# Two of eight weighted sums of a conditioning projection move from VectorE to TensorE in a fused mixer and MoE layer

## The chip, the cores and the metric

The kernel runs on one core of a Trainium2 chip. The time is device microseconds (us) of one execution, and the figure to compare is the median of several runs.

## The reference, cut to what matters

One layer of a decoder: 256 tokens of width 1024, float32. A condition vector `c` modulates both halves of the layer, then a mixer and a mixture of 32 experts (4 per token) follow.

```python
cond = jax.nn.silu(c)
mod = (cond @ w_ada[l] + b_ada[l])[:, None, :]                 # 1024 -> 6 * 1024
sh_m, sc_m, g_m, sh_f, sc_f, g_f = jnp.split(mod, 6, axis=-1)
h = modulate(rms_norm(x, norm_mix_g[l]), sh_m, sc_m)
x = x + g_m * hybrid_mixer(h, w_in[l], ..., w_out[l])
h = modulate(rms_norm(x, norm_ffn_g[l]), sh_f, sc_f)
y = moe_ffn(h.reshape(-1, d), router_w[l], ...)                # top 4 of 32 experts
x = x + g_f * y.reshape(bsz, seq, d)
return rms_norm(x, final_norm_g)
```

The change concerns the last third of `cond @ w_ada`: the 2048 columns that hold `sc_f` and `g_f`, a sum over 1024 rows.

## The kernel before, in words

**Two stages.** The mixer multiplies the tokens with `w_in` (7 sections of 1024 columns) and `w_out`. The experts then stream their weights, 6 units of 2 MB each, through 12 buffers. Nearly everything that is computed is small against the 466 MB that are read.

**The mixer's weights** come in units of 2 MB (or 1 MB, a "half") through four buffers R0 to R3 in `raw` and a few places aside; the list `homes` (L61) gives the order and the home of each. SP issues all loads in that order and waits before each until the former user of the place is done: for units of `w_in` on the semaphore `split_l`, for units of `w_ada` on `ada_used` (L412 to L440). A wait on SP holds every later load.

**Products.** ScalarE copies a weight piece rounded (`piece_high`, L627), VectorE makes the rest (`piece_low`, L831, which counts `split_l`), and TensorE takes three products per block (L1192). A step of the mixer is numbered m = 0 to 23: 2 column halves h, times 6 sections (`SC_C, SC_X, SC_B, GATE_A, U_, GATE_B`), times 2 pieces b. So m = 12 to 23 is h = 1, m = 18 and 19 are its GATE_A, m = 20 and 21 its U. The bank of step m is `B[m % 6]`. In iteration m VectorE and ScalarE first make piece m + 3, which needs TensorE to be through with step m, and then treat the bank of step m. The multiplication with `w_out` (L1423 with its helper L1192, banks `B[0]` to `B[3]`) follows step 23.

**The conditioning product on the side.** The first third is a TensorE product (`modulation`, L1222). The second is weighed on VectorE: each row of weights times its own scalar of `cT`, added up (`weigh`, L881 and L882), and TensorE adds the 128 partitions with a matrix of ones (`sum_weighed`, L1244). The last third comes in eight halves of 128 rows by 2048 columns: half 0 is weighed on ScalarE (L701), halves 1 to 7 on VectorE (`weigh_half`, L893), in the iterations that `HALF_AT` names (L78). The running sum is the left half of `spare`. After iteration 20 `sum_weighed(2)` adds its partitions into `B[0]` with 4 products, one for each 512 columns, which lie in four column groups of 32. VectorE then adds the bias (L826). Half 6 lies in the right half of `spare`, half 7 in the left half of R2.

**Hand over to the experts.** The first loads of expert weights wait on the end of the mixer. SP issues, in this order (L474 and on): load 0 once VectorE has made all pieces of U (`split_l`), load 1 once all halves are used (`ada_used` 16), the two pieces of `w_out`'s second half (L464) once the spatial products are done (`sp_done` 4), load 2 once `sum_weighed(2)` is done, load 3 once the pieces of GATE_B are made, load 4 and 5 on the first pieces of `w_out` and on step 23, load 6 on the last piece of the mixer's result, load 7 and 8 on parts of the `w_out` product, load 9 and 10 on its end (`mix_done` 4, the last product of TensorE in the mixer), and load 11 behind the router (`spread_out` 4). Each is 2 MB. After that each load waits for a buffer that TensorE releases (L1508 are the products of the experts).

Of the kernel before, what the change touches and what calls it, by code (L numbers as in the profile page):

```python
# [5 lines left out]
def hybrid_trunk(nc, x_in, c_in, w_ada, b_ada, norm_mix_g, w_in, conv_w, w_spatial, b_spatial, ln_v_g,  # L6
# [31 lines left out]
    KT = D // P  # L38
    HALF = 512
    NH = D // HALF  # L40
# [10 lines left out]
    SC_X, SC_B, SC_C, U_, V_, GATE_A, GATE_B = range(7)  # L51
# [23 lines left out]
    units = [u for u, _ in homes]  # L75
    TABLES_MIX, TABLES_FFN = ("ada", 1, 1), ("ada", 1, 2)
    WEIGH_AT = {1: 0, 4: 1, 7: 2, 9: 3}
    HALF_AT = {12: (1, 2), 13: (3,), 15: (4,), 16: (5,), 17: (6,), 18: (7,)}  # L78
    SUM_AT = {11: 1, 20: 2}
    HALVES = 2 * NS * NH  # L80
    split_units = [n for n, u in enumerate(units) if u[0] in ("in", "out")]
# [10 lines left out]
    unit_no = {u: n for n, u in enumerate(units)}  # L92
# [5 lines left out]
    with ctx:  # L98
# [3 lines left out]
        def sem(name):  # L102
            return ctx.enter_context(nc.semaphore(name))
# [20 lines left out]
        weighed = spare[:, 0:4 * HALF].rearrange("p (j n) -> p j n", j=4)  # L124
# [13 lines left out]
        def slot(n, k=1):  # L138
            return W[:, n * UW:(n + k) * UW]
# [12 lines left out]
        cond = late[:, 5 * P:5 * P + KT * 32].rearrange("p (k r) -> p k r", k=KT)  # L152
# [114 lines left out]
        ada_used = sem("ada_used"); weighed_ready = sem("weighed_ready"); ada_summed = sem("ada_summed"); ones_ready = sem("ones_ready"); split_h = sem("split_h"); split_l = sem("split_l")  # L267
# [15 lines left out]
        sec_act = sem("sec_act")  # L283
# [43 lines left out]
        def dve_bank(h, s, b):  # L327
            return dve_order.index((h, s, b)) + 1
# [4 lines left out]
        def act_bank(h, s, b):  # L333
            return act_order.index((h, s, b)) + 1

        def home(n):
            return homes[n][1]

        def raw_slot(n):
            if home(n) == ASIDE_SPARE:  # L340
                return spare[:, :]
            if home(n) == ASIDE_M:
                return slot(7)
            if home(n) == SPARE_RIGHT:
                return spare[:, UW // 2:UW]
            if home(n) in (R2_LEFT, R2_RIGHT):
                at = R2 * UW + (UW // 2 if home(n) == R2_RIGHT else 0)
                return raw[:, at:at + UW // 2]
            return raw[:, home(n) * UW:(home(n) + 1) * UW]

        def landed(n):
            return s_slot[home(n)], 16 * len([m for m in range(n + 1) if home(m) == home(n)])
# [22 lines left out]
        def sum_bank(i):  # L375
            return B[7] if i == 1 else B[0]
# [419 lines left out]
        def _(dve):  # L796
# [74 lines left out]
            def weigh(q):  # L871

                n = unit_no[("ada", 1, q)]
                dve.wait_ge(*landed(n))
                if q == 0:
                    dve.wait_ge(split_l, pieces_before[split_units.index(unit_no[("in", SC_X, 0)]) + 1])
                w = raw_slot(n).rearrange("p (k j n) -> p k j n", k=2, j=4)
                if q == 0:
                    step(V.tensor_scalar(weighed[:, :, :], w[:, 0], cT[:, 0:1], None, ALU.mult))
                else:  # L880
                    step(V.scalar_tensor_tensor(weighed[:, :, :], w[:, 0], cT[:, 2 * q:2 * q + 1], weighed[:, :, :], ALU.mult, ALU.add))  # L881
                V.scalar_tensor_tensor(weighed[:, :, :], w[:, 1], cT[:, 2 * q + 1:2 * q + 2], weighed[:, :, :], ALU.mult, ALU.add).then_inc(ada_used, 1)  # L882
                dve.wait_ge(ada_used, 4 + q + 1)
                if q == 3:
                    dve.nop().then_inc(weighed_ready, 1)

            def weigh_half(j):

                n = unit_no[("half", 2, j)]
                dve.wait_ge(*landed(n))  # L890
                dve.wait_ge(ada_used, 8 + j)
                sum_of = spare[:, 0:UW // 2]
                V.scalar_tensor_tensor(sum_of, raw_slot(n), cT[:, j:j + 1], sum_of, ALU.mult, ALU.add).then_inc(ada_used, 1)  # L893
                dve.wait_ge(ada_used, 8 + j + 1)
                if j == KT - 1:
                    dve.nop().then_inc(weighed_ready, 1)

            piece_low(V_ALL)
# [22 lines left out]
            for h in range(NH):  # L921
                for n, s in enumerate(SECTIONS):
                    for b in range(2):
                        m = 2 * (NS * h + n) + b
# [11 lines left out]
                        if s == SC_X:  # L936
# [6 lines left out]
                            for t in (2 * b, 2 * b + 1):  # L943
                                k = 4 * h + t
                                w = [cols[:, KT * (1 + j) + k:KT * (1 + j) + k + 1] for j in range(3)]
# [29 lines left out]
                        if m in WEIGH_AT:  # L975
                            weigh(WEIGH_AT[m])
                        for j in HALF_AT.get(m, ()):
                            weigh_half(j)
# [199 lines left out]
        def _(pe):  # L1178
            M = nc.tensor.matmul
# [3 lines left out]
            def arrived(n):  # L1183
                pe.wait_ge(*landed(n))

            def piece_ready(q):
                pe.wait_ge(split_l, q + 1)

            def product(o, k, left, right):

                for n, (i, j) in enumerate(((0, 0), (0, 1), (1, 0))):
                    t = M(o, left[i], right[j], start=(k == 0 and n == 0), stop=(k == KT - 1 and n == 2))  # L1192
                return t
# [31 lines left out]
            def turn_sums(part, g):  # L1225
# [4 lines left out]
                    t = M(first_bank(part, g)[:, q:q + 1], mod[:, g, P * q:P * q + P], row_sum, start=True, stop=True)  # L1230
                t.then_inc(modT_done, 1)

            def sum_weighed(i):

                if i == 1:
                    pe.wait_ge(wsT_ready, 2)
                    pe.wait_ge(ones_ready, 1)
                if i == 1:
                    pe.wait_ge(sp_used, 2)
                else:  # L1240
                    pe.wait_ge(sec_act, act_bank(NH - 1, GATE_A, 0))
                pe.wait_ge(weighed_ready, i)
                for j in range(4):
                    t = M(sum_bank(i)[32 * j:32 * j + 32, :], cond[:, 0, :], weighed[:, j, :], start=True, stop=True)  # L1244
                t.then_inc(ada_summed, 1)

            modulation(0, 0)
# [1 line left out]
            for k in range(KT):  # L1249
                for a in range(TA):  # L1250
                    c = T * (k % 2) + P * a
                    t = TR(B[k // 2][:, c:c + P], HV[:, a, k * P:(k + 1) * P], ident[:, :])
# [60 lines left out]
            def spatial(c):  # L1313

                if c == 0:
                    pe.wait_ge(v_ready, TA)
                    pe.wait_ge(wsT_ready, 2)
                if c >= 2:
                    pe.wait_ge(sp_used, c - 1)
                if c == 3:  # L1320
                    pe.wait_ge(mod_ready, 1)
                for g in (2 * c, 2 * c + 1):
                    for a in range(TA):
                        o = T * (g % 2) + P * a
                        t = M(B[6 + c % 2][:, o:o + P], HV[:, a, g * P:(g + 1) * P], wsT[:, g, :], start=True, stop=True)
                t.then_inc(sp_done, 1)


            for h in range(NH):
                for i, s in enumerate(SECTIONS):  # L1330
                    for b in range(2):
                        if s == U_ and b == 0:
                            spatial(2 * h)
                            spatial(2 * h + 1)
                        m = 2 * (NS * h + i) + b
                        if m >= 4 and m < 6:
                            pe.wait_ge(v_gelu, m - 3)
                        if m >= 6:
                            m0 = m - 6
                            h0, s0, b0 = m0 // (2 * NS), SECTIONS[(m0 // 2) % NS], m0 % 2  # L1340
                            if s0 in (SC_X, SC_B):
                                pe.wait_ge(sec_dve, dve_bank(h0, s0, b0))
                            else:
                                pe.wait_ge(sec_act, act_bank(h0, s0, b0))
                        q = V_ALL + m
                        piece_ready(q)
                        for tt in range(2):
                            for k in range(KT):
                                cs = slice(P * tt, P * tt + P)
                                t = product(B[m % 6][:, T * tt:T * tt + T], k, (in_set(wh, q)[:, k, cs], in_set(wl, q)[:, k, cs]),  # L1350
                                            (hh[:, k, :], hl[:, k, :]))
                        t.then_inc(sec_done, 1)
                        if m in SUM_AT:
                            sum_weighed(SUM_AT[m])
                    if s == SC_B and h == 0:
                        turn_spatial()
# [36 lines left out]
            for h in range(NH):  # L1393
                for ks in ((range(0, 4), range(4, 6), range(6, 8)) if h == 0 else (range(0, 4), range(4, 8))):
# [3 lines left out]
                    for a in range(TA):  # L1398
                        for k in ks:
# [3 lines left out]
                            t = product(B[TA * h + a][:, :], k, (mh[:, k, ts], ml[:, k, ts]), (rows_h[:, k % 4, :], rows_l[:, k % 4, :]))  # L1403
# [15 lines left out]
                    if h == 0 and ks[0] == 0:  # L1419
                        pe.wait_ge(sec_act, act_bank(NH - 1, GATE_B, 1))  # L1420
                        pe.wait_ge(sp_used, NG // 2)
                        for q in range(QW):
                            t = TR(B[6][:, P * q:P * q + P], mod[:, 1, P * q:P * q + P], ident[:, :])  # L1423
# [59 lines left out]
            for a in range(TA):  # L1483
                t = TR(B[7][:, a * P:(a + 1) * P], wts4[:, a, :], ident[:, :])
# [100 lines left out]
            n = pe.snap(rnd, min_val=0, max_val=ALL_ROUNDS)  # L1585
# [6 lines left out]
            n = pe.snap(rnd, min_val=0, max_val=ALL_ROUNDS)  # L1592
# [28 lines left out]
```

## Time and profile before

| | |
|---|---|
| median of 3 runs | 1139.98 us (1139.22 to 1141.19) |
| profiled execution, its own time | 1139.67 us |
| span of that execution in the profile | 1137.9 us |
| TensorE busy | 962.7 us (85%) |
| VectorE busy | 352.1 us (31%) |
| DMA queue of SP, share of the 16 engines | 98.8% |
| read from memory | 465.35 MB, 410 GB/s over the span |

The page gives busy time, a row of 40 slices (28.4 us each) for every engine, and the chain of waits that ended last. The busy shares say little alone, since the first 220 us and the rest are different programs; the slices and the chain, read against the order of loads above, tell which resource holds each stage.

### The profile page before, as it was taken

What the parts mean: (1) busy time and instruction counts of PE and PEld (TensorE: products, weight loads), DVE (VectorE), ACT (ScalarE), POOL (GpSimd) and SP (SyncE); (2) the same over time, 40 slices, a digit from 0 to 9 for tenths busy, and PEclk for the clock granted to TensorE, in tenths of its full rate; (3) what the DMA queues carried; (4) which work ended last, traced back from release to release, by engine and by line L of the source; (5) the groups of instructions that cost most, each with busy time, mean ns of one, the idle gap of its engine ahead of it and who ended that gap; (6) DMA issues with size and microseconds to landing.
All of it is one profiled execution on the core that took longest, in us unless ns stands there. A gap on an engine that the chain in (4) does not pass through costs nothing.

```text
span 1137.9 us, 24483 instructions
## 1 busy us (share of the span) xinstructions
PE 962.7 (85%) x10064; PEld 511.7 (45%) x10065; DVE 352.1 (31%) x799; ACT 248.1 (22%) x369; POOL 8.2 (1%) x30
## 2 busy tenths in 40 slices
PE   7999999989887997798898888989887687687664
PEld 6799999734332333243333334434333233233221
DVE  3688996752121222121222212212121121121112
ACT  3644535521011111010111101111010010111102
POOL 0010000000000000000000000000000000000000
PEclk9999999999999999899999999999989899899988
DMA  9999889999999999999999999999999999999996
GB/s 358 395 354 359 320 333 375 416 389 430 427 428 429 427 429 427 428 427 427 430 426 429 427 429 425 430 425 429 428 429 429 427 429 426 427 429 428 429 426 273
DMA packets 56094, 466.79 MB, mean 410 GB/s; under 512 B 5252, under 2 KB 6340, under 8 KB 27396
## 3 DMA queue, kind: packets, MB, share of 16 engines
q1 hardware_dynamic: 55808, 466.12, 98.8%
q8 instruction: 19, 0.31, 0.1%
q10 hardware_dynamic: 260, 0.30, 0.1%
q14 instruction: 7, 0.06, 0.0%
HBM read 465.35 MB, written 1.05 MB: 410 GB/s over the span
## 4 chain that ended last, share of the span: by engine, by line
PE 53%; DMA 39%; issue 3%; SPq 2%; DVE 1%; ACT 1%; PEld 0%; PEldq 0%; POOL 0%; POOLq 0%; DVEq 0%; ACTq 0%
PE B L1508 25%; DMA trio<-in_w_down_dram 25%; PE B L1192 14%; DMA W<-in_w_down_dram 10%; DMA W<-in_w_gate_up_dram 3%; PE B L1532 3%; PE B L1521 2%; SPq L474 2%; PE B L1460 2%; PE B L1271 1%; PE B L1466 1%; PE B L1199 1%; PE B L1280 1%; PE B L1222 0%; PE B L1566 0%
## 5 line engine op out<-in xcount | busy, mean ns | idle before, releaser
L1508 PE MATMUL B<-W,trio 128*32 128x512 f32 (+1 forms) x4768 | 469.9, 530 | 125.5 <-DMA W<-in_w_gate_up_dram 52.1
L1508 PEld LDWEIGHTS B<-W,trio 128*32 128x32 f32 x4768 | 154.9, 111 | 368.2 <-issue 225.0
L751 ACT ACTIVATE EW<-EW 128x256 f32<-128x256 f32 x46 | 19.1, 416 | 680.3 <-DVE EW L1124 680.3
L1124 DVE TENSOR_SCALAR EW<-B 128x256 f32<-128x256 f32 x46 | 19.5, 425 | 447.3 <-PE B L1508 447.3
L1192 PE MATMUL B<-hh,wh 128*128 128x256 f32 x384 | 109.1, 284 | 0.0
L1192 PE MATMUL B<-hl,wh 128*128 128x256 f32 x384 | 108.7, 283 | 0.0
L1192 PE MATMUL B<-hh,wl 128*128 128x256 f32 x384 | 108.7, 283 | 0.0
L1532 PE MATMUL B<-EW,trio 32*128 32x256 f32 x752 | 67.1, 426 | 8.7 <-PE B L1532 7.8
L1192 PEld LDWEIGHTS B<-hh,wh 128*128 128x128 f32 x384 | 73.7, 192 | 1.7 <-issue 1.7
L1192 PEld LDWEIGHTS B<-hl,wh 128*128 128x128 f32 x384 | 73.7, 192 | 0.0
L1192 PEld LDWEIGHTS B<-hh,wl 128*128 128x128 f32 x384 | 73.7, 192 | 0.0
L1139 DVE TENSOR_TENSOR EW<-B,trio 128x256 f32<-128x256 f32 x46 | 19.5, 425 | 164.7 <-PE B L1508 164.7
L627 ACT ACTIVATE wh<-raw 128x2048 fp32r<-128x2048 f32 (+1 forms) x30 | 50.3, 1690 | 83.0 <-PE B L1192 66.8
L831 DVE TENSOR_TENSOR wl<-raw,wh 128x2048 fp32r<-128x2048 f32 (+1 forms) x30 | 59.9, 2004 | 14.8 <-ACT wh L627 14.1
L1508 PE MATMUL B<-trio 128*32 128x256 f32 x768 | 48.6, 395 | 15.2 <-DMA trio<-in_w_down_dram 15.2
L751 ACT ACT_TABLE_LOAD x46 | 59.0, 1283 | 6.1 <-issue 5.3
L1521 PE MATMUL B<-b_gu,trio 128*32 128x256 f32 x736 | 56.4, 423 | 0.0
L1508 PE MATMUL B<-spare,trio 128*32 128x512 f32 x352 | 46.9, 647 | 8.2 <-DMA spare<-in_w_gate_up_dram 8.2
L1460 PE MATMUL B<-HV,trio 128*32 128x256 f32 x752 | 51.7, 388 | 0.0
L1532 PEld LDWEIGHTS B<-EW,trio 32*128 32x128 f32 x752 | 29.4, 182 | 47.4 <-PE B L1532 26.6
L1521 PEld LDWEIGHTS B<-b_gu,trio 128*32 128x32 f32 x736 | 29.3, 116 | 43.8 <-issue 38.0
L1460 PEld LDWEIGHTS B<-HV,trio 128*32 128x32 f32 x752 | 28.8, 113 | 38.9 <-issue 32.4
(259 smaller groups left out, 709.0 us busy)
## 6 DMA issues: line engine op xcount, KB each, us to landing
W<-in_w_gate_up_dram SPq DMA_DIRECT2D x112, 2048.0 KB, 33.7
W<-in_w_down_dram SPq DMA_DIRECT2D x48, 2048.0 KB, 37.4
spare<-in_w_gate_up_dram SPq DMA_DIRECT2D x16, 2048.0 KB, 37.1
trio<-in_w_down_dram SPq DMA_DIRECT2D x15, 2048.0 KB, 40.4
raw<-in_w_in_dram SPq DMA_DIRECT2D x10, 2048.0 KB, 14.5
raw<-in_w_ada_dram SPq DMA_DIRECT2D x4, 2048.0 KB, 16.9
raw<-in_w_ada_dram SPq DMA_DIRECT2D x7, 1024.0 KB, 11.8
raw<-in_w_in_dram SPq DMA_DIRECT2D x4, 1024.0 KB, 15.6
```

The lines of the kernel that those rows point to most:

```text
L474: sp.dma_start(unit_pair(u).rearrange("p g n -> p (g n)"), dn_v[e, j - NQ].rearrange("p g n -> p (g n)")).then_inc(s_unit[u % SLOTS], 16)
L627: A(in_set(wh, q), in_raw(q), ACT.Copy).then_inc(split_h, 1)
L751: A(sg, gs, ACT.Sigmoid, scale=ALPHA).then_inc(sig_ready, 1)
L831: V.tensor_tensor(in_set(wl, q), in_raw(q), in_set(wh, q).bitcast(f32), ALU.subtract).then_inc(split_l, 1)
L1124: V.tensor_scalar(halves(gs), paired(GU[:, 0:QC]), LIMIT, None, ALU.min).then_inc(gmin_ready, 1)
L1139: V.tensor_tensor(yw, Db[:, 0:QC], gfq, ALU.mult).then_inc(yw_ready, 1)
L1192: t = M(o, left[i], right[j], start=(k == 0 and n == 0), stop=(k == KT - 1 and n == 2))
L1199: TR(bank[:, 0:P], ident[:, :], ident[:, :])
L1460: t = M(Db[CAP * g:CAP * g + CAP, 0:QC], S[:, a, CAP * g:CAP * g + CAP], HV[:, a, g * QC:(g + 1) * QC], start=(a == 0), stop=(a == TA - 1))
L1508: t = M(o, src[:, k % KQ, CAP * (k // KQ):CAP * (k // KQ) + CAP], w, start=(k == 0), stop=(k == KT - 1))
L1521: M(GU[CAP * g:CAP * g + CAP, s * QC:(s + 1) * QC].rearrange("p (c q) -> p c q", q=KQ), sel[:, NH * s + g // 2, :], pairs[:, :, g % 2, :], ...
L1532: M(Yb[a][h][:, (g % 2) * QC:(g % 2) * QC + QC], SwT[rows_, a * P:(a + 1) * P], yw[rows_, :], start=False, stop=True, skip_group_check=Tru ...
```

## The change

Halves 6 and 7 are no longer weighed on VectorE. TensorE multiplies them with `cond` in 8 products (128 rows by 512 columns, in the same four column groups), straight into the bank that `sum_weighed(2)` adds to afterwards. They stand right behind the products of step 19, ahead of the spatial products. `ada_used` 15 and 16, for which SP waits, are now counted by TensorE. The running sum on VectorE is complete after half 5, and `sum_weighed(2)` adds to the bank in place of starting it.

```diff
-    HALF_AT = {12: (1, 2), 13: (3,), 15: (4,), 16: (5,), 17: (6,), 18: (7,)}
+    HALF_AT = {12: (1, 2), 13: (3,), 15: (4,), 16: (5,)}
+    PRODUCTS_OF, PRODUCTS_AT = (6, 7), 19
...
-                if j == KT - 1:
+                if j == PRODUCTS_OF[0] - 1:
                     dve.nop().then_inc(weighed_ready, 1)
...
+            def half_products():
+
+                pe.wait_ge(sec_act, act_bank(NH - 1, GATE_A, 0))
+                pe.wait_ge(ada_used, 8 + PRODUCTS_OF[0])
+                for j in PRODUCTS_OF:
+                    n = unit_no[("half", 2, j)]
+                    arrived(n)
+                    w = raw_slot(n).rearrange("p (i n) -> p i n", i=4)
+                    for i in range(4):
+                        t = M(sum_bank(2)[32 * i:32 * i + 32, :], cond[:, j, :], w[:, i, :], start=(j == PRODUCTS_OF[0]), stop=False)
+                    t.then_inc(ada_used, 1)
+
             def sum_weighed(i):
...
                 if i == 1:
                     pe.wait_ge(sp_used, 2)
-                else:
-                    pe.wait_ge(sec_act, act_bank(NH - 1, GATE_A, 0))
                 pe.wait_ge(weighed_ready, i)
                 for j in range(4):
-                    t = M(sum_bank(i)[32 * j:32 * j + 32, :], cond[:, 0, :], weighed[:, j, :], start=True, stop=True)
+                    t = M(sum_bank(i)[32 * j:32 * j + 32, :], cond[:, 0, :], weighed[:, j, :], start=(i == 1), stop=True)
                 t.then_inc(ada_summed, 1)
...
                         t.then_inc(sec_done, 1)
+                        if m == PRODUCTS_AT:
+                            half_products()
                         if m in SUM_AT:
                             sum_weighed(SUM_AT[m])
```

VectorE, iterations 17 to 19 (`spare` is the running sum, `wl` the piece that VectorE makes, L951 the bank of SC_B, L955 that of GATE_A), before:

```order
L951 TENSOR_TENSOR tmp<-tmp,B 128x512
L893 SCALAR_TENSOR_TENSOR spare<-spare,tmp 128x2048
L831 TENSOR_TENSOR wl<-raw,wh 128x2048
L955 TENSOR_TENSOR tmp<-tmp 128x512
L893 SCALAR_TENSOR_TENSOR spare<-raw,tmp,spare 128x2048
L831 TENSOR_TENSOR wl<-raw,wh 128x2048
L955 TENSOR_TENSOR tmp<-tmp 128x512
L831 TENSOR_TENSOR wl<-raw,wh 128x2048
```

and now (each line number is one higher):

```order
L952 TENSOR_TENSOR tmp<-tmp,B 128x512
L832 TENSOR_TENSOR wl<-raw,wh 128x2048
L956 TENSOR_TENSOR tmp<-tmp 128x512
L832 TENSOR_TENSOR wl<-raw,wh 128x2048
L956 TENSOR_TENSOR tmp<-tmp 128x512
L832 TENSOR_TENSOR wl<-raw,wh 128x2048
```

The two weighings are gone; each stood ahead of a piece that SP or TensorE waits for. TensorE from the last product of step 19 to the first of step 20, before (`B<-tmp,HV` are the spatial products):

```order
L1192 MATMUL B<-hh,wl 128x256
L1325 MATMUL B<-tmp,HV 128x128 [waits sp_used]
L1325 MATMUL B<-tmp,HV 128x128 x3
L1325 MATMUL B<-tmp,HV 128x128 [waits mod_ready,sp_used]
L1325 MATMUL B<-tmp,HV 128x128 x3
L1192 MATMUL B<-hh,wh 128x256 [waits split_l,sec_dve]
```

and now (`s_slot8` is the landing of half 6, `s_slot6` that of half 7):

```order
L1193 MATMUL B<-hh,wl 128x256
L1243 MATMUL B<-spare,tmp 32x512 [waits s_slot8,ada_used,sec_act]
L1243 MATMUL B<-spare,tmp 32x512 x3
L1243 MATMUL B<-raw,tmp 32x512 [waits s_slot6]
L1243 MATMUL B<-raw,tmp 32x512 x3
L1336 MATMUL B<-tmp,HV 128x128 [waits sp_used]
L1336 MATMUL B<-tmp,HV 128x128 x3
L1336 MATMUL B<-tmp,HV 128x128 [waits mod_ready,sp_used]
L1336 MATMUL B<-tmp,HV 128x128 x3
L1193 MATMUL B<-hh,wh 128x256 [waits split_l,sec_dve]
```

Eight products stand ahead of all that follows on TensorE, with three new kinds of wait.

## Rows read from the trace of the kernel before

**Rows 1.** The page: DMA rate in 40 slices of 28.4 us.
```profile
GB/s 358 395 354 359 320 333 375 416 389 430 427 428 429 427 429 427 428 427 427 430 426 429 427 429 425 430 425 429 428 429 429 427 429 426 427 429 428 429 426 273
```
**Rows 2.** The chain that ended last, in order of time: start us, us, what.
```profile
30.30 1.85 PE B L1222 x16
...
124.30 46.27 PE B L1192 x384
...
170.57 1.79 PE B L1325 x16
...
178.10 0.99 PE B L1244 x8
...
235.04 3.00 PE B L1508 x16
...
269.14 33.45 DMA trio<-in_w_down_dram
```
**Rows 3.** Timeline of VectorE, 162 to 175 us.
```profile
162.02 2.35 DVE L893 SCALAR_TENSOR_TENSOR spare<-raw,tmp,spare 128x2048 f32<-128x2048 f32 x1
...
167.33 2.35 DVE L893 SCALAR_TENSOR_TENSOR spare<-spare,tmp 128x2048 f32<-128x2048 f32 x1
169.72 2.29 DVE L831 TENSOR_TENSOR wl<-raw,wh 128x2048 fp32r<-128x2048 f32 x1
...
172.53 2.34 DVE L893 SCALAR_TENSOR_TENSOR spare<-raw,tmp,spare 128x2048 f32<-128x2048 f32 x1
```
**Rows 4.** Timeline of ScalarE: the piece of iteration 18 and the bank of step 18.
```profile
164.90 1.92 ACT L627 ACTIVATE wh<-raw 128x2048 fp32r<-128x2048 f32 x1 [3.84 <-PE B L1192]
166.73 0.58 ACT L696 ACTIVATE tmp<-B 128x512 f32<-128x512 f32 x1
```
**Rows 5.** Timeline of TensorE around `sum_weighed(2)`.
```profile
177.70 0.28 PE L1192 MATMUL B<-hl,wh 128*128 128x256 f32 x1
177.82 0.28 PE L1192 MATMUL B<-hh,wl 128*128 128x256 f32 x1
178.03 1.06 PE L1244 MATMUL B<-spare,tmp 128*32 128x512 f32 x8
...
179.25 0.28 PE L1192 MATMUL B<-hl,wh 128*128 128x256 f32 x1
```
**Rows 6.** Timeline of SP: half 7, loads 0, 1, 8, 9 and 11.
```profile
159.08 0.33 SPq L440 DMA_DIRECT2D raw<-in_w_ada_dram  x1
...
172.03 0.33 SPq L470 DMA_DIRECT2D W<-in_w_gate_up_dram  x1
...
174.90 0.33 SPq L470 DMA_DIRECT2D W<-in_w_gate_up_dram  x1
...
216.00 0.33 SPq L470 DMA_DIRECT2D W<-in_w_gate_up_dram  x1
...
222.36 0.33 SPq L470 DMA_DIRECT2D W<-in_w_gate_up_dram  x1
...
231.58 0.67 SPq L472 DMA_DIRECT2D trio<-in_w_down_dram  x1
```
**Rows 7.** DMA issues, us to landing: half 7, loads 0, 8, 9, 11.
```profile
raw<-in_w_ada_dram SPq DMA_DIRECT2D x1, 1024.0 KB, 5.0
...
W<-in_w_gate_up_dram SPq DMA_DIRECT2D x1, 2048.0 KB, 7.7
...
W<-in_w_gate_up_dram SPq DMA_DIRECT2D x1, 2048.0 KB, 9.9
...
W<-in_w_gate_up_dram SPq DMA_DIRECT2D x1, 2048.0 KB, 8.9
...
trio<-in_w_down_dram SPq DMA_DIRECT2D x1, 2048.0 KB, 10.0
```
**Rows 8.** Busy time by stretch; the last number is the DMA rate in GB/s.
```profile
170.00:175.00 5.00, 5.00 (x45) 5.00 (x44) 4.87 (x3) 2.52 (x2) 0.00 (x0) 1.00 0.42 108
220.00:225.00 5.00, 4.78 (x47) 3.64 (x46) 3.06 (x6) 2.66 (x8) 0.00 (x0) 1.00 0.97 360
```

## The prediction, on record before the changed kernel ran

> **What bounds the kernel now.** I read the slices first. From slice 9 on the DMA rate stays at 425 to 430 GB/s, while before it, in the mixer, it lies between 320 and 416 [rows 1]. So the experts' stage (some 880 us of it) runs at the rate of the loads, and nothing that TensorE or VectorE saves there counts. What counts is when this stream gets going and whether it is ever interrupted before.
>
> Next the chain of waits [rows 2]. Through the second half of the mixer it runs on TensorE alone: 46.27 us without a break for steps 12 to 19 (384 products in 46.1 us is 5.76 us a step), the spatial products and `sum_weighed(2)`, each followed by further steps. The end of the `w_out` product sends load 9 at 222.36 [rows 6]. TensorE starts the first expert at 235.04, and only at 269.14 does the chain pass to a load, one that takes 33.45 us to land behind the loads queued ahead of it. Up to about 245 us the loads are issued as TensorE gets on; after that they queue and the rate alone decides.
>
> Then VectorE around the change [rows 3]. It weighs half 6 at 167.33 (2.35 us) and only then makes its piece of iteration 18 at 169.72, though ScalarE's part of that piece was ready at 164.90 + 1.92 = 166.82 [rows 4]. It weighs half 7 at 172.53, to 174.87. SP waits for both: load 0 goes out at 172.03, as the piece ends, and load 1 at 174.90, as half 7 is weighed [rows 3, 6]. The queue has run dry by then, with 108 GB/s between 170 and 175 us [rows 8]. That is the hole which this change can fill.
>
> **What the change removes.** Two VectorE operations, 2.35 + 2.34 = 4.7 us. The piece of iteration 18 can start at 167.33 in place of 169.72, so load 0 goes out 2.4 us earlier, at 169.65. The next piece waits for ScalarE, whose step needs TensorE's step 19 anyway; TensorE never waited for a piece in this stretch (its 5.76 us a step has no gap), so VectorE's freed time gives TensorE nothing.
>
> **What it adds on TensorE.** Eight products of 128 by 512 in column groups, which the trace lists as 16 records. The nearest row is `sum_weighed(2)`: four of the same form, 8 records. Without them the last product at 177.82 would be followed 0.12 us later by the next (the distance from the row before), and one product after that stands at 179.25. So 179.25 - 177.82 - 2 x 0.12 = 1.19 us is the whole price of four, both changes of form included [rows 5]. `modulation` has eight such products at 1.85 us, against 0.99 us for four [rows 2], so four more cost 0.86 us. Together 1.19 + 0.86 = **2.05 us**. From below the price is 1.85 us, the eight alone; from above it is 2 x 1.19 = 2.4 us, if half 6 and half 7 are paid for like two separate groups. I take 2.05, since the two stand back to back as in `modulation`.
>
> The Trainium skill (TensorEngine Tiling (Array Packing), Key Properties) says that changing the tiling mode drains TensorE, which speaks against putting short products in column groups between full ones. By the rows above the two changes and the drain are worth 1.19 - 0.86 = 0.33 us, which the sum has. The page gives no figure for it, so by the rule alone the term could not be sized.
>
> **Waits.** All that the eight products wait for is long there when step 19 ends at 170.4: half 5 is weighed at 162.02 + 2.35 = 164.4 [rows 3], the bank of step 18 is read at 167.3 [rows 4], half 7 has landed at 159.08 + 5.0 = 164.1 [rows 6, 7], and half 6 was there at 167.33, when VectorE took it [rows 3]. I price them at nothing. If one were late, it would hold the spatial products, the remaining steps and everything else on TensorE.
>
> **What moves.** The products end near 172.4, where `ada_used` reaches 16; load 1 leaves at about 172.6, 2.3 us earlier than now. The `w_out` pieces then wait for the spatial products, which end at 172.4 now [rows 2] and at 174.4 then, still ahead of load 1's present 174.9. Load 2 waits for `sum_weighed(2)` and is later by 2.05, after 181.1 in place of 179.1 [rows 2]; it is covered by loads 0 and 1 and the `w_out` pieces, 6 MB or about 15 us. Everything that waits for a later step of TensorE, loads 3 to 11 and the router among it, moves back by 2.05 us.
>
> **The sum.** Does the stream feel the 2.4 us gained at load 0, or the 2.05 us lost behind it? Load 8 goes out at 216.00 and lands at 225.9; load 9 goes out at 222.36, on the last product of TensorE in the mixer, and lands at 231.3 [rows 6, 7]. That is 5.4 us apart, where 2 MB at 427 GB/s take 4.9, and the rate in that stretch falls to 360 GB/s [rows 8]. Load 11 goes out at 231.58 and lands at 241.6, where two loads of 4.9 us behind load 9 would be down at 231.3 + 9.8 = 241.1. So both come late already today: what the queue had been given earlier is used up by load 9, and the head start of 2.4 us only makes it wait longer there. From load 9 on the whole stream moves with TensorE. Terms: VectorE 0 (hidden under TensorE's steps), load 0 and 1 0 (spent before load 9), TensorE +2.05, router and experts 0. The profiled execution of 1139.67 us would come to 1141.7; the median lies 0.3 above that execution, so I predict **1142.0 us**, with 1141.8 to 1142.4 by the bounds of the one term, and 0.6 us of scatter on either side, as runs lie up to 1.2 us above their median.
>
> **Rivals.**
>
> *The wait is hidden at load 9.* Load 0, into an empty queue, landed in 7.7 us [rows 7]. If load 9 needs no more than that, it lands at 222.36 + 2.05 + 7.7 = 232.1, 0.8 us later than now and not 2.05. With load 11 soaking up some of it in the same way, the sum lies between 0 and +0.8: 1140.0 to 1140.8. For it: 8.9 is more than 7.7. Against it: the dip in rate at 220 to 225, and load 11, which again comes late and is again tied to TensorE. The Trainium skill (DMA: Bandwidth & Descriptors, Anatomy of one DMA) fits the gpsimd path with 2.0 us plus bytes over 436 GB/s, 6.8 us for 2 MB as an estimate; by that load 9 would land at 231.2, just as now, and the change would cost nothing. SP's loads here need 7.7 us even alone. Chance 0.16.
>
> *The head start carries.* If the late landings of loads 9 and 11 are only a lower rate of the engines and not late issues, then the queue holds work throughout, and all later loads keep the 2.3 us that loads 0 and 1 gain: 1139.98 - 2.3 = 1137.7 us, faster. It decides from the point where load 4 to load 9 never find the queue short. Against it: load 9's lead over the landing of load 8 is 3.5 us now and would be no larger than that. Chance 0.07.
>
> *The products cost more in this place, and the kernel is slower.* Between step 19 and step 20 stand three kinds of products in a row now, half 6, half 7 behind a landing wait and a count of its own, and the spatial ones. If the overlap breaks at each of the three borders and each costs what the break at `sum_weighed(2)` costs, it is 3 x 1.19 = 3.6 us: 1143.6. It decides from 2.3 us on, where the shift exceeds what can be told. For it: none of the rows has such a sequence. Against it: `modulation` runs eight such products in 1.85 us, and its two groups of four overlap. Chance 0.11. That the change doesn't do what it says isn't likely: the order shows 8 products more and 2 weighings fewer.
>
> **How the numbers follow.** This measurement can tell about 0.2%, 2.28 us: slower begins at 1142.26. The forecast has 0.66, and with its scatter a third of that lies above the line, 0.22. Slower is 0.22 + 0.10 = 0.32, same 0.44 + 0.16 + 0.02 = 0.62, faster 0.06. The range takes in the hidden case down to 1139.6 and the forecast with part of the dearer case up to 1143.4; left out are the faster case and the dearest part.
>
> **What would show it.** L1243 as 16 records in about 1.9 us right behind step 19; step 20 starting near 174.2; load 0 at 169.6 and load 1 near 172.6; `sum_weighed(2)` at 180.1; the end of the `w_out` product at 224.4 and the first expert at 237.1; load 9 landing near 233.3. The forecast is wrong if TensorE's shift at step 20 is not about 2 us, or if the shift at load 9's landing is under 1 us or vanishes by load 12's.

## The result, and the profile after

| | before | after |
|---|---|---|
| median of 20 runs each | 1140.03 us (1138.08 to 1141.29) | 1141.4 us (1140.56 to 1148.18) |
| ratio, with its 95% interval | | 1.0016 (1.001 to 1.0023) |
| profiled execution, span | 1137.9 us | 1140.0 us |
| TensorE, VectorE busy | 962.7, 352.1 us | 962.3, 347.4 us |

The ratio is 1.8 us (1.1 to 2.6), the medians lie 1.4 us apart. The kernel is a little slower, within the 0.2% that the prediction called no change; 1142.0 us had been forecast.

The chain that ended last in the changed kernel, in order of time (start us, us, what):

```profile
124.35 46.27 PE B L1193 x384
170.62 1.85 PE B L1243 x16
172.47 1.98 PE B L1336 x16
174.45 5.74 PE B L1193 x48
...
181.19 22.94 PE B L1193 x168
...
237.07 3.48 PE B L1521 x16
...
270.97 34.05 DMA trio<-in_w_down_dram
```

Against [rows 2]: steps 12 to 19 take the same 46.27 us, then the eight products stand in the chain with 1.85 us, the spatial products take 1.98 in place of 1.79, and the first expert starts at 237.07, 2.03 us later. The pass to a load comes at 270.97 in place of 269.14.

VectorE in the changed kernel, the stretch of [rows 3]:

```profile
162.07 2.35 DVE L894 SCALAR_TENSOR_TENSOR spare<-raw,tmp,spare 128x2048 f32<-128x2048 f32 x1
164.57 2.29 DVE L832 TENSOR_TENSOR wl<-raw,wh 128x2048 fp32r<-128x2048 f32 x1 [0.15 <-DVE spare L894]
...
167.49 2.29 DVE L832 TENSOR_TENSOR wl<-raw,wh 128x2048 fp32r<-128x2048 f32 x1
...
172.66 2.29 DVE L832 TENSOR_TENSOR wl<-raw,wh 128x2048 fp32r<-128x2048 f32 x1 [2.27 <-ACT wh L628]
```

The piece of iteration 18 starts at 167.49 in place of 169.72. The next one now waits 2.27 us for ScalarE, as VectorE has caught up: what was freed there turns into idle time.

SP's issues in the changed kernel (loads 0, 1, 2, 8, 9, 11, 12):

```profile
169.81 0.33 SPq L471 DMA_DIRECT2D W<-in_w_gate_up_dram  x1
...
172.53 0.33 SPq L471 DMA_DIRECT2D W<-in_w_gate_up_dram  x1
...
181.25 0.34 SPq L471 DMA_DIRECT2D spare<-in_w_gate_up_dram  x1
...
218.09 0.33 SPq L471 DMA_DIRECT2D W<-in_w_gate_up_dram  x1
...
224.46 0.33 SPq L471 DMA_DIRECT2D W<-in_w_gate_up_dram  x1
...
233.67 0.67 SPq L473 DMA_DIRECT2D trio<-in_w_down_dram  x1
...
240.59 0.34 SPq L471 DMA_DIRECT2D W<-in_w_gate_up_dram  x1
```

and the times to landing of loads 8, 9, 11 and 12 among them (last number, us):

```profile
W<-in_w_gate_up_dram SPq DMA_DIRECT2D x1, 2048.0 KB, 8.6
...
W<-in_w_gate_up_dram SPq DMA_DIRECT2D x1, 2048.0 KB, 8.2
...
trio<-in_w_down_dram SPq DMA_DIRECT2D x1, 2048.0 KB, 9.9
...
W<-in_w_gate_up_dram SPq DMA_DIRECT2D x1, 2048.0 KB, 10.2
```

Loads 0 and 1 go out 2.22 and 2.37 us earlier than in [rows 6]; loads 8, 9 and 11 each 2.1 us later. Load 9 lands at 224.46 + 8.2 = 232.7, only 1.4 us later than before, load 11 at 243.6, 2.0 us later, and load 12 at 250.8, 2.1 us later. From there on both profiles keep 4.9 us a load, but for 0.3 us more at load 14 in the changed kernel.

Busy time by stretch in the changed kernel (last number: DMA rate, GB/s):

```profile
170.00:175.00 5.00, 5.00 (x44) 3.43 (x43) 2.73 (x3) 2.40 (x2) 0.00 (x0) 1.00 0.84 289
...
195.00:200.00 5.00, 5.00 (x38) 4.74 (x37) 3.58 (x3) 3.06 (x3) 0.00 (x0) 1.00 0.69 216
...
225.00:230.00 5.00, 4.78 (x52) 3.70 (x44) 4.02 (x15) 3.56 (x8) 0.54 (x2) 1.00 0.95 328
```

The hole of 108 GB/s at 170 to 175 us [rows 8] is filled, 289 GB/s; a new one opens at 195 to 200, 216 GB/s where the kernel before had 426, ahead of load 4. Load 4 waits for TensorE's later steps, so the hole was moved by 25 us and not removed.

### The profile page after: what moved, and what is told of

It is laid out like the page before. It is cut to its first block, busy times and chain, and to the rows that moved or that the text cites. A ratio compares the mean times of both kernels' runs of the same rounds, so it can differ in the third digit from the quotient of the medians.

```text
span 1140.0 us, 24510 instructions
## 1 busy us (share of the span) xinstructions
PE 962.3 (84%) x10080; PEld 511.6 (45%) x10081; DVE 347.4 (30%) x797; ACT 247.9 (22%) x369; POOL 8.2 (1%) x30
## 4 chain that ended last, share of the span: by engine, by line
PE 52%; DMA 40%; issue 3%; SPq 3%; DVE 1%; ACT 0%; PEld 0%; PEldq 0%; DVEq 0%; ACTq 0%
DMA trio<-in_w_down_dram 25%; PE B L1521 25%; PE B L1193 14%; DMA W<-in_w_down_dram 10%; DMA W<-in_w_gate_up_dram 3%; PE B L1545 3%; SPq L475 2%; PE B L1534 2%; PE B L1473 2%; PE B L1282 1%; PE B L1479 1%; DMA raw<-in_w_ada_dram 1%; PE B L1223 1%; SPq L471 1%; PE B L1291 1%
```

## The experiments

Two theories are tried. Mine: what the loads need is TensorE's progress to load 9 and beyond, each us on its path costs one, and the earlier issue of loads 0 and 1 is worth nothing. The rival: the head start carries, and the change would have won without its products' price.

All moments in this table are counted so that the first product of `sum_weighed(1)` stands at 123.23 us, as in the profile before, since whole profiles are shifted by up to 5.5 us by what goes on before step 12 (in the experiments, too, that changed nothing there; the last section shows what goes with it). "Clock" is the lowest clock, as a share of the full one, that TensorE was granted in the first 2 us of the first expert. Ratio and interval are against the kernel before on the same chip; each row of moments is from one profile.

| kernel | load 0 out | load 8 lands | load 9 out, lands | load 12 out, lands | clock | median us | ratio |
|---|---|---|---|---|---|---|---|
| before | 172.0 | 225.9 | 222.4, 231.3 | 238.1, 248.7 | 0.50 | 1140.03 | 1 |
| after | 169.8 | 226.6 | 224.4, 232.6 | 240.5, 250.7 | 0.50 | 1141.4 | 1.0016 (1.001 to 1.0023) |
| r2_products_added | 172.0 | 227.5 | 224.4, 233.8 | 239.0, 249.8 | 1.00 | 1142.03 | 1.0008 (0.9998 to 1.0018) |
| r4_weigh_later | 169.7 | 223.8 | 222.4, 230.8 | 237.1, 247.4 | 1.00 | 1139.78 | 0.9995 (0.9986 to 1.0005) |
| r1_no_products | 169.8 | 224.2 | 222.4, 230.3 | 237.0, 247.9 | 1.00 | 1139.83 | 0.9995 (0.9985 to 1.0005) |
| r3_products_twice | 169.8 | 228.7 | 226.1, 233.8 | 240.8, 251.3 | 1.00 | 1143.44 | 1.0026 (1.0017 to 1.0036) |
| r9_products_five_times | 169.8 | 234.5 | 231.3, 239.5 | 247.0, 257.0 | 1.00 | 1148.76 | 1.0078 (1.0062 to 1.0093) |
| r6_products_at_20 | 169.8 | 228.8 | 224.1, 233.5 | 238.7, 248.3 | 1.00 | 1141.11 | 1.0005 (0.9995 to 1.0016) |
| r7_turns_behind | 172.1 | 225.3 | 221.4, 230.2 | 238.7, 248.3 | 0.50 | 1138.28 | 0.9988 (0.9977 to 0.9999) |
| r12_turns_again | 172.1 | 225.4 | 221.4, 230.5 | 237.3, 247.6 | 1.00 | 1139.29 | 0.9992 (0.9977 to 1.0008) |
| r8_turns_and_weigh | 169.7 | 224.9 | 221.4, 231.4 | 238.2, 247.2 | 0.50 | 1139.75 | 0.9999 (0.9990 to 1.0009) |
| r10_kept_warm | 172.0 | 225.3 | 222.4, 231.2 | 237.1, 247.7 | 1.00 | 1139.48 | 0.9992 (0.9981 to 1.0003) |
| r11_turns_and_warm | 172.0 | 225.5 | 221.4, 230.4 | 237.3, 247.0 | 1.00 | 1138.65 | 0.9989 (0.9974 to 1.0003) |

What a profile has gained or lost against the profile before at load 12's landing, it keeps. At the landing of load 170 of 192 the distance is the same within 0.3 us in every profile but one: 2.0 and 2.1 us later in the changed kernel, 8.3 and 8.2 later in r9, 1.3 and 1.4 earlier in r4. In r11 0.8 of 1.7 us is lost again, 0.7 of it at load 14. r8, r9 and r12 lose another 1.2 to 1.5 us at load 181, for a reason that was not found. So load 12's landing is the moment by which the rows are best compared, and only among rows of one clock. The time from its issue to its landing differs from profile to profile by up to 1.9 us (9.0 to 10.9), so a difference of less than 1 us between two rows says little.

### The cost alone: r2_products_added

```diff
 (kernel before)
                         t.then_inc(sec_done, 1)
+                        if m == 19:
+                            pe.wait_ge(sec_act, act_bank(NH - 1, GATE_A, 0))
+                            for j in (6, 7):
+                                for i in range(4):
+                                    M(sum_bank(2)[32 * i:32 * i + 32, :], cond[:, j, :], HV[:, i % 2, HALF * (i // 2):HALF * (i // 2) + HALF], start=(j == 6), stop=(j == 7))
```

> The kernel before, all seven halves still weighed on VectorE, with eight more products of the same form (128x512 in four column groups) on TensorE behind step 19, on other data (the normalised v), into a bank that sum_weighed(2) starts anew. The cost alone, without the head start of loads 0 and 1. My theory (the loads from 9 on follow TensorE, the head start is spent before them): load 0 at 172.0 and load 1 at 174.9 as before, step 20 about 2.0 us later, load 9 landing 1.4 to 2.0 us later, load 12 2.0 to 2.3 us later, time +1.5 to +2.1 us, the same as the whole change. Rival (the head start carries part of the time): dearer than the whole change by up to 2.3 us, so +3 to +4 us.

The chain of r2_products_added, in order of time:

```profile
170.77 1.85 PE B L1357 x16
172.63 1.98 PE B L1325 x16
174.61 5.74 PE B L1192 x48
```

The same 1.85 and 1.98 us as in the changed kernel, and load 9 goes out 2.0 us later. With no head start it lands 2.5 us later, more than the 1.4 us of the changed kernel and than the 2.0 us that I had allowed, so the head start does reach load 9 in part. Load 12 lands 1.1 us later than in the profile before and 2.1 to 2.4 later than in the profiles of r4 and r10, which have its clock. The time, +0.9 us by the ratio (-0.2 to +2.1) and +1.8 by the medians, is no more than the change's. I had expected +1.5 to +2.1, which the interval still holds; the rival's +3 us lies outside it.

### The head start of load 0 alone: r4_weigh_later

```diff
-    HALF_AT = {..., 17: (6,), 18: (7,)}
+    HALF_AT = {..., 18: (6, 7)}
```

> The kernel before with half 6 weighed one iteration later, behind the piece of iteration 18, so that load 0 goes out about 2.3 us earlier and TensorE does nothing more. The head start of load 0 alone. My theory: load 0 near 169.7, load 1 within 0.3 us of 174.9, load 9 issued and landed as before within 0.3 us, time 0 within 0.6 us. Rival (the head start carries): load 9 and all later ones land 1 to 2.3 us earlier, time -1 to -2.3 us.

Load 0 leaves at 169.7 and load 9 at the same moment as before; load 8 lands 2.1 us earlier. Of these 2.1 us, 0.5 is left at load 9's landing. Load 12 lands 1.3 us earlier, but 1.0 of that is there at its issue already, from another cause (r10, below). The time doesn't move: -0.6 us (-1.6 to +0.6). A gain of 2.3 us is excluded, one of half a us is not.

### Both head starts without the cost: r1_no_products

```diff
 (changed kernel, in half_products)
                     arrived(n)
-                    w = raw_slot(n).rearrange("p (i n) -> p i n", i=4)
-                    for i in range(4):
-                        t = M(sum_bank(2)[32 * i:32 * i + 32, :], cond[:, j, :], w[:, i, :], start=(j == PRODUCTS_OF[0]), stop=False)
-                    t.then_inc(ada_used, 1)
+                    pe.nop().then_inc(ada_used, 1)
...
-                    t = M(sum_bank(i)[32 * j:32 * j + 32, :], cond[:, 0, :], weighed[:, j, :], start=(i == 1), stop=True)
+                    t = M(sum_bank(i)[32 * j:32 * j + 32, :], cond[:, 0, :], weighed[:, j, :], start=True, stop=True)
```

> The changed kernel without the eight products: TensorE counts halves 6 and 7 as used when they have landed, and their share of the last third of the conditioning is left out. The modulation before the router differs, so tokens may go to other experts and the number of rounds may change; the loads up to the first expert are comparable, the time only if the rounds are. Both head starts without the cost. My theory: load 0 near 169.8, load 1 near 170.6, load 9 issued at 222.3 to 222.5 and landed within 0.5 us of 231.3, load 12 within 0.5 us of 248.7, time 0 within 0.7 us if the rounds are the same. Rival (the head start carries): load 9 lands at 229 to 230 and load 12 2 to 4 us earlier, time -2 to -4 us.

SP's issues of loads 8, 9 and 12 in r1_no_products, and their times to landing:

```profile
217.95 0.33 SPq L471 DMA_DIRECT2D W<-in_w_gate_up_dram  x1
...
224.32 0.33 SPq L471 DMA_DIRECT2D W<-in_w_gate_up_dram  x1
...
238.98 0.34 SPq L471 DMA_DIRECT2D W<-in_w_gate_up_dram  x1
```

```profile
W<-in_w_gate_up_dram SPq DMA_DIRECT2D x1, 2048.0 KB, 8.2
...
W<-in_w_gate_up_dram SPq DMA_DIRECT2D x1, 2048.0 KB, 7.9
...
W<-in_w_gate_up_dram SPq DMA_DIRECT2D x1, 2048.0 KB, 10.9
```

Less 1.96 us for this profile's shift, load 8 lands at 224.2 and load 9 at 230.3, 1.0 us earlier than before: 7.9 us after its issue, not the 8.9 us of [rows 7]. My theory had allowed 0.5 us there, so this step was missed: the kernel before did have about 1 us of slack at load 9. But load 12 takes 10.9 us from its issue and lands 0.8 us earlier, again with 1.1 us of another cause in its issue, and the time is -0.6 us (-1.7 to +0.6). The trace has 24063 instructions in place of 24483, as tokens go to other experts, so the time alone wouldn't settle it; together with r4 it does. At the full clock load 12 lands at 247.4 in r4, at 247.9 in r1 and at 247.7 in r10, which has no head start at all. The head start of 2.3 us is gone by load 12.

### The price doubled and taken five times: r3_products_twice, r9_products_five_times

```diff
 (changed kernel, in half_products; r9 the same with four turns for nothing)
                     w = raw_slot(n).rearrange("p (i n) -> p i n", i=4)
                     for i in range(4):
+                        M(sum_bank(2)[32 * i:32 * i + 32, :], cond[:, j, :], w[:, i, :], start=True, stop=True)
+                for j in PRODUCTS_OF:
+                    w = raw_slot(unit_no[("half", 2, j)]).rearrange("p (i n) -> p i n", i=4)
+                    for i in range(4):
                         t = M(sum_bank(2)[32 * i:32 * i + 32, :], cond[:, j, :], w[:, i, :], start=(j == PRODUCTS_OF[0]), stop=False)
```

> The changed kernel with the eight products done twice, the first time for nothing. My theory: 32 records in 3.6 us, load 9 issued and load 12 landed another 1.7 to 1.8 us later than with the change, time +3.3 to +3.9 us against the kernel before, that is twice the change's cost less one pair of changes of form. Rival (a wait for the halves, not the products, set the change's cost): less than 0.5 us more than the change.

> The changed kernel with the eight products five times, four of them for nothing: 80 records. My theory: 1.85 + 4 x 1.72 = 8.7 us of products on TensorE, load 9 issued 6.9 us later than with the change, the stream after it moves by as much: +6.9 us against the change, +8.3 to +9.1 us against the kernel before. Rival (part of TensorE's delay is taken up by the queue of loads or by the experts' stage): under +7 us against the kernel before.

The chain of r3_products_twice and that of r9_products_five_times:

```profile
170.92 1.85 PE B L1243 x16
172.77 1.72 PE B L1247 x16
```

```profile
172.28 8.72 PE B L1245 x80
```

A repetition costs 1.72 us, five turns 8.72. Load 9 goes out 1.7 us later than with the change in r3 and 6.9 us later in r9. The time goes up by 3.0 us (1.9 to 4.1) and by 8.9 us (7.1 to 10.6) against the kernel before; the products add 3.6 + 0.2 and 8.7 + 0.2 us to TensorE's path by these rows. So no taking up of the delay is seen: in r9 it is one for one, to within the 1.8 us of its interval. Between the change and r3 lie 1.1 us by the ratios where 1.7 were expected, within their intervals.

Load 12 lands only 0.6 us later in r3 than with the change, where 1.7 to 1.8 were expected, but the changed kernel's profile has the fallen clock and that of r3 has not. Among the rows at the full clock it lands at 247.4 to 247.9 without products on TensorE's path (r4, r10, r1), at 249.8 with eight (r2), at 251.3 with sixteen (r3) and at 257.0 with forty (r9, whose router took 1.0 us longer as well, with the clock fallen there). That is 1.9 to 2.4, 3.4 to 3.9 and 9.1 to 9.6 us later, where TensorE's rows give 2.0, 3.8 and 8.9 + 1.0.

### One change of form for all twelve: r6_products_at_20

```diff
-    PRODUCTS_OF, PRODUCTS_AT = (6, 7), 19
+    PRODUCTS_OF, PRODUCTS_AT = (6, 7), 20
```

> The changed kernel with the eight products one step later, behind step 20 and directly ahead of the four products of sum_weighed(2), so that one change of form there and back serves all twelve. Load 0 keeps its head start, load 1 waits until about 180 and loses 5 us against the kernel before. My theory: the twelve cost TensorE 0.99 + 1.72 us and one pair of changes, 0.2 to 0.3 us less than the change does; load 1 lands near 188, load 8 near 226 to 227, load 9 (issued near 224.1) within 0.5 us of where the change has it; time +1.3 to +2.1 us against the kernel before. Rival (loads 1 to 8 matter): load 1 being 5 to 7 us later shows in load 9's landing by more than 1.5 us, time +3 us and more.

The chain of r6_products_at_20:

```profile
129.75 46.27 PE B L1193 x384
...
186.26 22.94 PE B L1193 x168
```

From the start of step 12 to that of step 21 it takes 186.26 - 129.75 = 56.51 us; in the kernel before 54.80 (124.30 to 178.10 + 0.99 and the start of the next step at 179.10), in the changed one 181.19 - 124.35 = 56.84. The eight products cost 1.71 us here and 2.04 there, so one change of form there and back is 0.33 us, just as the rows of before gave it. Load 1 leaves 5 us later than in the kernel before and 7.5 later than in the changed one. Load 9 lands 0.9 us later than in the changed one, above the 0.5 expected. Load 12 lands at 248.3, no later than in r2 (249.8), which has the full clock too. The time is +0.6 us (-0.6 to +1.8), which excludes the rival's +3. That loads 1 to 8 have several us of slack up to load 12 is shown; that this place is better than the change's is likely by the 0.33 us, but not shown by the time.

### TensorE's path made shorter: r7_turns_behind, r12_turns_again, r8_turns_and_weigh

```diff
 (kernel before, TensorE; ScalarE's copies move likewise)
-                        if h == NH - 1 and a == 0 and ks[0] == 4:
-                            pe.wait_ge(xs_ready, TA)
-                            for a2 in range(TA):
-                                turn_x(0, a2)
...
+            pe.wait_ge(xs_ready, TA)
+            for a2 in range(TA):
+                turn_x(0, a2)
             pe.wait_ge(xs_ready, TA + 1)
             turn_x(1, 0)
```

> The kernel before with eight transposes (turn_x(0, .), 0.87 us), which stand within the w_out product, moved behind its end, and ScalarE's copies of them moved back likewise. TensorE reaches the issue of loads 9 and 10 0.87 us earlier without any work less. My theory: load 9 issued 0.8 to 0.9 us earlier after the start of step 12, first expert 0.3 to 0.9 us earlier, load 12 landing 0.3 to 0.9 us earlier, time -0.3 to -0.9 us. Rival (TensorE's path to load 9 has slack): load 12 and the time within 0.2 us of the kernel before.

> r7 together with half 6 weighed one iteration later (r4): the loads of r4 and the issue of load 9 of r7. My theory: the time of r7 less up to 0.4 us, since an earlier load 8 leaves load 9 nearer to its least time to landing, -0.5 to -1.2 us against the kernel before. Rival (both act on nothing): within 0.2 us.

> r7 once more, for its time alone (0.9988, 0.9977 to 0.9999, at first). My theory: 0.9990 to 0.9997, that is -0.3 to -1.1 us. Rival (scatter): an interval that holds 1 and a median within 0.3 us of the kernel before.

Load 9 goes out 0.9 to 1.0 us earlier in all three and lands 0.8 to 1.1 us earlier in r7 and r12. In r8 it took 10.0 us and landed as before, at 231.4, though load 8 was early there. The first expert starts no earlier: at 235.24, 235.23 and 235.26 after the shift, against 235.04 before. The expected gain there didn't come; the transposes and ScalarE's copies of them are now ahead of the router, which would explain it. Load 11 goes out 0.2 us later (231.8). The times of r7, r12 and r8 are -1.4 us (-2.6 to -0.1), -0.9 (-2.6 to +0.9) and -0.1 (-1.1 to +1.0). One interval lies below 1 and the others hold it; r8 came out as its rival had it (within 0.2 us) and not at the -0.5 to -1.2 that I expected. At load 12 r7 is 0.4 us ahead of the profile before, which has the same clock, r8 1.5 us (of which 1.2 are lost at load 181), and r12 lies between r4 and r10. So a gain by this edit is possible and not shown.

### TensorE kept at its full clock ahead of the first expert: r10_kept_warm, r11_turns_and_warm

```diff
             gather()
+            keep_warm(2, B[5])
...
             t.then_inc(wT_done, 1)
+            keep_warm(8, B[6])
```

> The kernel before with ten transposes of the identity, for nothing, into unused banks: two behind the gather and eight ahead of the first expert's products, where TensorE stands idle for 1.3 us. In five of ten profiles so far TensorE's granted clock fell to 0.50 for about 3 us there, and load 12 went out 1 us later after the start of step 12 than in the others. My theory (load 12 is issued as TensorE lets go of its first unit and takes 10 to 11 us, so the stream follows that moment): granted clock 1.00 from 234 to 242 us, load 12 issued at 237.0 to 237.3 counted from the start of step 12 as in the profile before, time -0.3 to -1.0 us. Rival (load 12's moment doesn't matter): time within 0.2 us of the kernel before.

> r7 and r10 together. My theory: load 9 issued 0.85 us earlier and load 12 1 to 1.5 us earlier than in the profile before, counted from step 12; time -0.8 to -1.8 us. Rival (r7's gain was scatter): time within 0.3 us of r10.

Busy time by stretch in the profile before, at the first expert; the third number from the end is TensorE's granted clock:

```profile
235.00:236.00 1.00, 0.95 (x8) 0.30 (x12) 0.88 (x6) 0.00 (x0) 0.00 (x0) 0.91 0.70 229
236.00:237.00 1.00, 1.00 (x12) 0.27 (x5) 0.88 (x6) 0.00 (x0) 0.00 (x0) 0.50 1.01 369
237.00:238.00 1.00, 1.00 (x12) 0.32 (x8) 0.86 (x7) 0.00 (x0) 0.00 (x0) 0.50 0.92 377
```

and in r10_kept_warm, whose first expert starts at 237.05:

```profile
236.00:238.00 2.00, 1.58 (x18) 0.71 (x20) 1.81 (x11) 0.18 (x1) 0.00 (x0) 1.00 0.83 258
238.00:240.00 2.00, 2.00 (x32) 1.01 (x28) 1.74 (x12) 0.00 (x0) 0.00 (x0) 1.00 1.01 373
240.00:242.00 2.00, 2.00 (x21) 0.58 (x16) 1.28 (x11) 0.51 (x1) 0.00 (x0) 1.00 1.08 451
```

At the half level (0.50, that is 1.2 of 2.4 GHz) the first 16 records take 3.00 us in the profile before [rows 2] and 3.48 after; at the full level they take 2.00 in r2_products_added:

```profile
237.17 2.00 PE B L1513 x16
```

Load 12 goes out 1.0 us later in the profile before than in r4, r1 and r10, which have the full clock and the same path, and lands 0.8 to 1.3 us later. r7 and r12 are one kernel: with the fallen clock load 12 goes out at 238.7 and lands at 248.3, without it at 237.3 and 247.6. So load 12 moves with the moment at which TensorE lets go of its first unit. The times, -0.9 us (-2.2 to +0.3) and -1.3 (-3.0 to +0.3), lie on the side of the theory and don't show a gain. Profiles at the full clock come without the transposes too, so these two don't show that the transposes brought it.

## Why the prediction was right

**The price on TensorE** was the term that carried the sum, 2.05 us. Step 21 starts 56.84 us after step 12 in place of 54.80: 2.04 us. The products took 1.85 us, and the spatial products behind them 0.19 us more. A repetition of the eight took 1.72, so 0.32 us go to the two changes of form around them. The Trainium skill (TensorEngine Tiling (Array Packing), Key Properties) says that changing the tiling mode drains TensorE; the trace agrees that it costs, 0.33 us there and back by r6.

**The waits** were priced at nothing, and the products start at 170.62, as step 19 ends. Step 20 starts at 174.45: [rows 2] and 2.05 us give 174.4, and the 174.2 in the prediction's list of signs was a slip.

**VectorE** gave 4.7 us and TensorE got nothing of it, as priced: its steps keep their 5.76 us, and VectorE now waits 2.27 us for ScalarE.

**Loads 0 and 1** left at 169.81 and 172.53, where 169.65 and 172.6 had been worked out, and this head start was worth nothing that the times of r4 and r1 can tell.

**Where the stream is tied to TensorE** was put too early. "From load 9 on the whole stream moves with TensorE" isn't right for load 9: its landing moved by 1.4 us and not 2.05, in r1 it came 7.9 us after its issue and not 8.9. Here the rival of the hidden wait had the better mechanism, a wait of up to 1 us at load 9 that a head start can take away (the shortest time to landing there was 7.7 us, in r3). But it stops at load 11, which landed 2.0 us later, and load 12 settles the matter, which I had left out of the working: issued as TensorE lets go of the first expert's first unit, it took 9.0 to 10.9 us in the profiles here, and landed 2.0 us later with the change. The size of the sum came out right because load 12 is tied to TensorE as I took load 9 to be. In so far as no row of the prediction had looked at load 12, that was luck. r9 shows the tie in time, 8.7 us of products and 8.9 us of time (7.1 to 10.6).

**The median** lies 1.4 us above that of before, the ratio says 1.8, the sum had 2.05; both lie within the term and the scatter given for it.

## What to carry to other kernels

In a kernel whose second stage is bound by loads, an earlier load is worth something only if no later load of the same queue is tied to the slower path; follow the queue to its last load that is issued late, and price the change there. Here work taken from VectorE, which the critical engine didn't wait for, bought nothing that can be told, and the same work on TensorE, which everything waits for, cost its full duration. Before moving such work, look whether it can share a change of form with a neighbour: here that was 0.33 of 2.04 us.

## What the runs showed of the hardware that was not expected

TensorE's granted clock fell to 0.50 for 3.4 us at the first expert in 4 of 13 profiles (before, after, r7 and r8, 0.2 to 0.9 us behind its first product) and within the router in r9. It stayed at 1.00 there in the others, among them kernels with the same instructions. Ahead of the first expert TensorE had been idle for 1.29 us in the profile before, and also for 1.27 us in that of r4, which kept 1.00:

```profile
235.04 3.00 PE L1508 MATMUL B<-W,trio 128*32 128x512 f32 x16 [1.29 <-issue]
```

```profile
236.64 2.04 PE L1508 MATMUL B<-W,trio 128*32 128x512 f32 x16 [1.27 <-issue]
```

So the idle time there alone doesn't decide it. What does was not found. Such a fall sends load 12 out 1.0 to 1.4 us later, half of what this change costs or more.

The larger shifts between profiles come from the start of the mixer. Six profiles (r1, r4, r6, r9, r10, r12) reach `sum_weighed(1)` 1.6 to 5.5 us later than the profile before, and all six show a clock of 0.50 between 12 and 30 us for longer or later than the rest: at 23 us (r1, r4, r9, r12), for 6.8 us (r10), or for 10.2 and once more for 3.4 us (r6). The other seven show none, or one of 3.4 us from 12 us on, and are shifted by 0.4 us at most. The sixteen products that stand at 23 us take, in the profile before and in that of r4 with its fall from 23.3 to 26.7:

```profile
22.73 3.94 PE B L1271 x16
```

```profile
22.82 5.54 PE B L1271 x16
```

The 1.6 us between them are r4's whole shift, and as large as what most of these experiments try to tell apart. That such falls widen the intervals of the times is likely, and not shown, since only one run of each kernel was profiled. What brings them was not found.
